# Two more load buffers for the first experts, an identity product for the last group's token sums, and the sample rows normalised in 128 partitions

## The reference, cut to what matters

```python
grp_prob = softmax(tok @ w_gr + b_gr)            # 4 groups of 8 experts, the best group is taken
top_w, top_e = the two best experts in that group
hid = silu(tok @ w_g[e]) * (tok @ w_u[e])        # 32 experts, 2048 -> 256, f32
out = sum over e of combine[:, e] * (hid @ w_d[e])
ple = sigmoid(h @ w_ple_gate) * (p @ w_ple_proj)
x_new = layer_norm(ALPHA * h + out + ple, ln2_g, ln2_b)   # (256, 2048) and (8, 2048)
```

## Time and profile before

| | us |
|---|---|
| median of 3 runs | 1445.55 |
| lowest and highest of them | 1442.3, 1449.25 |
| the profiled execution's own time | 1442.14 |
| its span, first to last instruction | 1440.2 |
| granted TensorE clock, mean of the span | 0.964 |

### The profile page before, as it was taken

The page is one execution under the profiler, slowest core; times in us unless marked ns, Lnnn a source line. Parts: engine busy times, 40 slices in busy tenths (PEclk is TensorE's granted clock), DMA queues, the critical chain, the costliest instruction groups (busy, mean ns, idle before and its releaser), DMA issues.

```text
span 1440.2 us, 21521 instructions
## 1 busy us (share of the span) xinstructions
PE 1320.1 (92%) x8977; PEld 1028.1 (71%) x8977; DVE 762.1 (53%) x1252; ACT 374.4 (26%) x547; POOL 93.9 (7%) x99
## 2 busy tenths in 40 slices
PE   7989999999999999999999998999988799998772
PEld 6989899998788788799999984655543256575320
DVE  4778989898785385465674474012042122211238
ACT  3424333331111211353343462310012020111110
POOL 3840000000010100100100001000000000000000
PEclk9989999999999999999999998999999899999897
DMA  9434444444343633555654649999999999998991
GB/s 249 149 116 154 159 156 147 147 147 144 121 139 127 207 113 108 192 163 187 195 176 147 239 171 357 402 368 403 407 409 408 409 387 398 407 394 321 409 350 71
DMA packets 140534, 351.16 MB, mean 244 GB/s; under 512 B 20808, under 2 KB 21936, under 8 KB 140424
## 3 DMA queue, kind: packets, MB, share of 16 engines
q1 hardware_dynamic: 137168, 339.36, 64.8%
q0 software_dynamic: 3264, 10.37, 2.3%
HBM read 342.52 MB, written 7.18 MB: 243 GB/s over the span
## 4 chain that ended last, share of the span: by engine, by line
PE 69%; DVE 13%; DMA 11%; issue 3%; ACT 2%; SPq 1%; POOL 0%; DVEq 0%; ACTq 0%; POOLq 0%
PE bank L553 67%; DMA mslot<-in_w_exp_up 5%; DMA mslot<-in_w_exp_down 3%; DVE lo L1706 2%; DVE wA L1872 2%; DVE atok L2533 1%; SPq L1247 1%; DVE xpair L1878 1%; ACT hi L1403 1%; DVE wB L1879 1%; DMA raw<-in_w_in 1%; DMA out<-stS 1%; DVE xpair L1881 1%; DVE wA L1891 1%; DMA out<-Sf 1%
## 5 line engine op out<-in xcount | busy, mean ns | idle before, releaser
L1706 DVE TENSOR_TENSOR lo<-raw,hi 128x2048 fp32r<-128x2048 f32 x80 | 188.8, 2361 | 112.0 <-ACT hi L1403 111.5
L1403 ACT ACTIVATE hi<-raw 128x2048 fp32r<-128x2048 f32 x79 | 151.3, 1915 | 258.2 <-PE bank L553 258.2
L553 PE MATMUL bank<-XT,raw 128*128 128x264 f32 x896 | 212.5, 391 | 0.8 <-ACT GA L1500 0.8
L553 PE MATMUL bank<-XH,hi 128*128 128x264 f32 x704 | 206.2, 293 | 5.3 <-DVE lo L1706 5.2
L553 PE MATMUL bank<-XL,hi 128*128 128x264 f32 x704 | 202.0, 287 | 0.0
L553 PE MATMUL bank<-XH,lo 128*128 128x264 f32 x704 | 201.0, 285 | 0.0
L553 PEld LDWEIGHTS bank<-XT,raw 128*128 128x128 f32 x896 | 167.4, 191 | 32.0 <-issue 4.1
L553 PE MATMUL bank<-mslot,Xg 128*32 128x512 f32 (+1 forms) x1024 | 146.9, 663 | 31.5 <-DMA mslot<-in_w_exp_up 31.5
L553 PEld LDWEIGHTS bank<-XH,hi 128*128 128x128 f32 x704 | 134.5, 191 | 11.6 <-DVE lo L1706 7.2
L553 PEld LDWEIGHTS bank<-XL,hi 128*128 128x128 f32 x704 | 134.5, 191 | 0.0
L553 PEld LDWEIGHTS bank<-XH,lo 128*128 128x128 f32 x704 | 134.2, 191 | 0.0
(11 more groups left out here) (421 smaller groups left out, 2101.1 us busy)
## 6 DMA issues: line engine op xcount, KB each, us to landing
raw<-in_w_in SPq DMA_DIRECT2D x72, 1024.0 KB, 5.1
mslot<-in_w_exp_gate SPq DMA_DIRECT2D x128, 512.0 KB, 10.3
mslot<-in_w_exp_up SPq DMA_DIRECT2D x128, 512.0 KB, 12.1
mslot<-in_w_exp_down SPq DMA_DIRECT2D x60, 1024.0 KB, 14.4
raw<-in_w_out SPq DMA_DIRECT2D x16, 1024.0 KB, 5.0
mslot<-in_w_ple_gate SPq DMA_DIRECT2D x16, 1024.0 KB, 13.9
raw<-in_w_branch_b SPq DMA_DIRECT2D x8, 1024.0 KB, 5.0
raw<-in_w_branch_a SPq DMA_DIRECT2D x8, 1024.0 KB, 5.2
```

What stands on the lines that cost most here:

```text
L553: return nc.tensor.matmul(out, w, x, start=start, stop=stop)
L1403: nc.scalar.activation(hi[:, s % RH, :], raw[:, n % RD, :], ACT.Copy).then_inc(hi_done, 1)
L1706: v.tensor_tensor(lo[:, n % RD, :], raw[:, n % RD, :], hi[:, s % RH, :].bitcast(F32), ALU.subtract).then_inc(lo_done, 1)
```

## The change

Four edits:

1. Two buffers are added behind the ten (`EXTRA = 2`), in the space of the second and third tile of `atok`. Chunks 10 and 11 go there, once; from chunk 12 on the ten old buffers are used in turn (`lane`). Chunks 12 to 21 therefore wait for `m_used` to reach two less than before, and later ones for what they waited for before. GpSimd clears `atok` only when 12 chunks have been used, and the filler products `keep_clock` read another buffer.
2. In the last group of the experts TensorE puts the old token sums into the side bank by a product with the identity (`last_scatter`), adds the group's result on top of them, and ScalarE copies the finished sum to `atok` (`copy_sums`); VectorE only takes the statistics (`last_statistics`).
3. The 8 sample rows are spread over 128 partitions (16 to a row) by an SBUF to SBUF transfer `srows<-atok`; their mean and deviation are spread by a small product (`ssel`, `sscal`); two instructions on 128x128 take the place of four on 8x1024.
4. For that, GpSimd's queue issues 17 small loads (`ssel`, 4 KB, and 16 pieces `svecs` of 8 KB each in SBUF) once the last `ple` result has been transposed.

```diff
+EXTRA = 2
...
-        [R_GAB + 8192 * q for q in range(4)] + [R_RAW + 8192 * q for q in range(4)] + [R_HI, R_HI + 8192])]
+        [R_GAB + 8192 * q for q in range(4)] + [R_RAW + 8192 * q for q in range(4)] + [R_HI, R_HI + 8192] +
+        [R_Z + 8192 * (q + 1) for q in range(EXTRA)])]
...
+        def lane(c):
+            return c if c < RM + EXTRA else (c - EXTRA) % RM
-            eng.wait_ge(m_land[c % RM], sum(m_size[x] for x in range(c % RM, c + 1, RM)))
+            eng.wait_ge(m_land[lane(c)], sum(m_size[x] for x in range(c + 1) if lane(x) == lane(c)))
...
-                    mm(bank[0][:, 0:NT], MH[:, i % 4, 0:128], MH[:, i % 4, :], True, True)
+                    mm(bank[0][:, 0:NT], ML[:, i % 4, 0:128], ML[:, i % 4, :], True, True)
...
+            def last_scatter(g, nb):
+                cs = slice(nb * 512, (nb + 1) * 512)
+                if nb == 0:
+                    stored(("st", 0, g))
+                banks = []
+                for tt, (t0, tn) in enumerate(TOK):
+                    banks.append(side(("sc", 0, g, nb, tt)))
+                    stored(("sc", 0, g - 1, nb, tt))
+                    mm(banks[tt][0:tn, :], ident[0:tn, 0:tn], atok[0:tn, tt, cs], True, False)
+                pe.wait_ge(out_low, 4 * g + nb + 1)
+                for tt, (t0, tn) in enumerate(TOK):
+                    mm(banks[tt][0:tn, :], SelT[:, g % 2, t0:t0 + tn], outh[:, nb % 2, :], False, False)
+                    mm(banks[tt][0:tn, :], SelT[:, g % 2, t0:t0 + tn], outl[:, nb % 2, :], False,
+                       True).then_inc(misc_ready, 1)
...
-                down(rnd, groups - 1, lambda nb: scatter(rnd, groups - 1, nb))
+                if rnd:
+                    down(rnd, groups - 1, lambda nb: scatter(rnd, groups - 1, nb))
+                else:
+                    down(rnd, groups - 1, lambda nb: last_scatter(groups - 1, nb))
...
+            def spread_sample_scalars(again):
+                b = side(("samples", again))
+                pe.wait_ge(f_vecs, 16 * 17)
+                pe.wait_ge(f_spread, again + 1)
+                mm(b[:, 0:2], ssel[:, :], sscal[:, :], True, True).then_inc(misc_ready, 1)
+            spread_sample_scalars(0)
+                spread_sample_scalars(1)
...
-                if c >= RM:
+                if c >= 2 * RM + EXTRA:
+                elif c >= RM + EXTRA:
+                    sp.wait_ge(m_used, c - RM - EXTRA + 1)
+                elif c >= RM:
+                    sp.wait_ge(chunk_used, N_END)
...
-                for tt, (t0, tn) in enumerate(TOK):
-                    dst = outs[0][0, t0:t0 + tn, :] if tt < 2 else outs[1].rearrange("b a d -> (b a) d")
-                    for half in range(2 if tt < 2 else 1):
-                        cs = slice(1024 * half, 1024 * (half + 1)) if tt < 2 else slice(0, D)
-                        sp.wait_ge(f_out, 6 * again + (2 * tt + half + 1 if tt < 2 else 6))
+                sp.wait_ge(f_turned, again + 1)
+                sp.dma_start(srows[:, :], atok[0:NB, 2, :]).then_inc(f_small, 16)
+                for tt, (t0, tn) in enumerate(TOK[0:2]):
+                    dst = outs[0][0, t0:t0 + tn, :]
+                    for half in range(2):
+                        cs = slice(1024 * half, 1024 * (half + 1))
+                        sp.wait_ge(f_out, 5 * again + 2 * tt + half + 1)
+                sp.wait_ge(f_out, 5 * again + 5)
+                sp.dma_start(outs[1].rearrange("b a (c j) -> (b a c) j", c=16), syn[:, :]).then_inc(y_out, 16)
...
+            pool.wait_ge(m_used, RM + EXTRA)
+            pool.wait_ge(misc_ready, misc["ple", 3, 2][0] + 1)
+            pool.dma_start(ssel[:, :], t["consts"][0:NB, C_SEL:C_SEL + 128]).then_inc(f_vecs, 16)
+            for i, n in enumerate(("ln2_gain", "ln2_bias")):
+                for b in range(NB):
+                    pool.dma_start(svecs[16 * b:16 * b + 16, i, :], t[n][0].rearrange("(c j) -> c j", c=16)).then_inc(
+                        f_vecs, 16)
...
+            def copy_sums(g, nb):
+                for tt, (t0, tn) in enumerate(TOK):
+                    b, read = side(("sc", 0, g, nb, tt))
+                    nc.scalar.activation(atok[0:tn, tt, nb * 512:(nb + 1) * 512], b[0:tn, :],
+                                         ACT.Copy).then_inc(read, 1)
+            def last_store(g):
+                for nb in range(4):
+                    down_done(act, 0, g, nb)
+                    if nb < 2:
+                        act.wait_ge(misc_ready, misc["sc", 0, g - 1, nb + 2, 2][0] + 1)
+                    nc.scalar.activation(outh[:, nb % 2, :], bank[nb][:, :], ACT.Copy).then_inc(out_high, 1)
+                    if nb:
+                        for done in ((0, 1) if nb == 1 else (nb,)):
+                            copy_sums(g, done)
...
-                store(rnd, groups - 1)
+                if rnd:
+                    store(rnd, groups - 1)
+                else:
+                    last_store(groups - 1)
...
+            def last_statistics(g, nb):
+                for tt, (t0, tn) in enumerate(TOK):
+                    side_read(dve, ("sc", 0, g, nb, tt))
+                    final_link(v.bn_stats(stats[0:tn, tt, nb, :], atok[0:tn, tt, nb * 512:(nb + 1) * 512]))
...
-                scatter(0, g, 0)
-                scatter(0, g, 1)
-                side_read(dve, ("sc", 0, g, 0, 2))
-                side_read(dve, ("sc", 0, g, 0, 1))
-                side_read(dve, ("sc", 0, g, 0, 0))
-                row_statistics(0)
+                last_statistics(g, 0)
+                last_statistics(g, 1)
-                for tt in range(3):
-                    side_read(dve, ("sc", 0, g, 1, tt))
-                row_statistics(1)
-                scatter(0, g, 2)
+                last_statistics(g, 2)
-                for tt in range(3):
-                    side_read(dve, ("sc", 0, g, 2, tt))
-                row_statistics(2)
-                scatter(0, g, 3)
-                row_statistics(3)
+                last_statistics(g, 3)
+                v.memset(told, 0.0).then_inc(f_turned, 1)
...
+                final_link(v.tensor_copy(sscal[:, 0:1], mv[0:NB, 2, 0:1]))
+                v.tensor_copy(sscal[:, 1:2], rstd[0:NB, 2:3]).then_inc(f_spread, 1)
-                for tt, (t0, tn) in enumerate(TOK):
+                for tt, (t0, tn) in enumerate(TOK[0:2]):
...
-                                dve.wait_ge(gained, 6 * again + 2 * tt + half + 1)
+                                dve.wait_ge(gained, 5 * again + 2 * tt + half + 1)
+                b, read = side(("samples", again))
+                v.tensor_copy(sums2[:, :], b[:, 0:2]).then_inc(read, 1)
+                dve.wait_ge(f_small, 16 * again + 16)
+                dve.wait_ge(f_vecs, 16 * 17)
+                side_read(dve, ("samples", again))
+                v.scalar_tensor_tensor(out=syn[:, :], in0=srows[:, :], scalar=sums2[:, 0:1], in1=svecs[:, 0, :],
+                                       op0=ALU.subtract, op1=ALU.mult).then_inc(gained, 1)
+                dve.wait_ge(gained, 5 * again + 5)
+                v.scalar_tensor_tensor(out=syn[:, :], in0=syn[:, :], scalar=sums2[:, 1:2], in1=svecs[:, 1, :],
+                                       op0=ALU.mult, op1=ALU.add).then_inc(f_out, 1)
...
```

More of the change, by code:

```diff
@@ L58 @@
 C_MASK = 400
-C_END = C_MASK + 8 * 128
+C_SEL = C_MASK + 8 * 128
+C_END = C_SEL + 128
 def shape_constants():
@@ L72, in shape_constants @@
     c[:, C_MASK:C_MASK + 128] = np.eye(128)
+    c[0:NB, C_SEL:C_SEL + 128] = r[None, :] // 16 == np.arange(NB)[:, None]
     for n, w in enumerate(LEVELS):
@@ L264, in build @@
     logT = at("logT", R_Z + 40960, [36, NT])
+    srows = at("srows", R_AR + 50272, [P, 128])
+    syn = at("syn", R_AR + 50272 + 512, [P, 128])
+    svecs = at("svecs", R_AR + 50272 + 1024, [P, 2, 128])
+    ssel = at("ssel", R_AR + 49216, [NB, 128])
+    sums2 = at("sums2", R_AR + 49216 + 544, [P, 2])
+    sscal = at("sscal", R_AR + 49216 + 512, [NB, 2])
     wrb = at("wrb", R_AR + 43264, [P, KD, 36])
@@ L331, in build @@
         landed = [sem(f"chunk_landed{s}") for s in range(RD)]
-        m_land = [sem(f"expert_chunk_landed{n}") for n in range(RM)]
+        m_land = [sem(f"expert_chunk_landed{n}") for n in range(RM + EXTRA)]
         hi_done, lo_done, chunk_used = sem("high_done"), sem("low_done"), sem("chunk_used")
@@ L368, in build @@
         gained = sem("gained")
+        f_spread, f_turned, f_small = sem("sample_scalars_ready"), sem("sample_rows_spread"), sem("sample_rows_stored")
+        f_vecs = sem("spread_gain_and_bias_loaded")
         norm_act = sem("normalized")
@@ L933, in ple_gate @@
                     for k in range(4):
-                        last = mm(bank[m][:, 0:NT], mslot[c % RM][:, k * 512 + m * 128:k * 512 + (m + 1) * 128],
+                        last = mm(bank[m][:, 0:NT], mslot[lane(c)][:, k * 512 + m * 128:k * 512 + (m + 1) * 128],
                                   HT[:, 4 * kq + k], kq == 0 and k == 0, kq == 3 and k == 3)
@@ L1225, in ple_load @@
```

(8 more changed lines are left out.)

18 lines of the change are left out of this document (9 added, 9 removed).

## The result

| | us |
|---|---|
| kernel before, median of 8 runs (1440.77 to 1449.25) | 1442.69 |
| changed kernel, median of 8 runs (1433.77 to 1439.02) | 1435.71 |
| ratio, with its 95% interval | 0.9949 [0.9931, 0.9967] |
| profiled execution of the changed kernel, and its span | 1439.02, 1437.2 |

The change makes the kernel 0.5% faster, 7.0 us by these medians. With 8 runs in place of 3 the median of the kernel before is itself 2.9 us lower than the one that the forecast started from.

What follows compares the result with a forecast made beforehand. The prediction took DMA and TensorE in turns as the expert stage's bound, then TensorE, VectorE and the last store. -5.3 + 2.9 + 0.3 - 3.2 + 1.0 = -4.3 us gave 1437.8, plus 3.4: 1441 us, range 1436 to 1447.

Steps and rivals of the forecast that it cites:

- the empty window: Just ahead of the expert stage, 852 to 864 us, DMA share 0.01; two chunks loading there save 5.3 us.
- group 1's first wait: Products at 896.05 us wait for chunks landing 5.3 us earlier; the wait was to stay one for DMA.
- The step at full clock in group 1: Last of the slow steps after waits takes 3.64 us, not 5.34: 1.7 us sooner, so -7.0 us for the buffers.
- The clears: GpSimd's three clears of `atok`, 5.30 us, move some 5 us later, covered by group 0's work: 0.
- the waits were filled as said: In the tail, identity products fill TensorE's three waits ahead of scatters, 1.67 + 1.69 + 1.52 = 4.9 us.
- the upper bound of +3.9 us: Identity sums in the tail: 10.9 us of products, no small waits regained, 0.3 us more of signals.
- The lower bound: Identity sums in the tail: +2.0 us, with 10.2 us of products.
- the first rival: Whole kernel, everything at its good end: -8.2 us, 1437 us; chance 0.20.
- The table load: In the tail, 1.28 us, starting only after the last copy; at most 0.2 us of it shows.
- the rival by which the change is slower: TensorE's clock falls in the tail, from 1400.35 us on; 20.8 us of work doubles, 1462 us; chance 0.04.
- the bound of -3.8 us: Sample rows at the kernel's end: 4.85 us become 1.0 us and the small store does not queue.
- a price by bytes (0.3) and one by packets (2.0): Seventeen small loads near 1325 us: 0.135 MB at 403 GB/s cost 0.3 us, 264 packets cost 2.0 us; +1.0 us taken.

Runs made afterwards that it cites:

- run 9: The changed kernel with one extra buffer (`EXTRA = 1`) in place of two; median 1439.11 us, 1.0 us under the kernel before.
- runs 7 and 11: Changed kernel with the small loads issued after the last group's first down products, 1437.00 us; changed kernel with identity sums for the last 512 columns only, 1430.59 us.
- run 8: The changed kernel with identity sums for the last 512 columns only; median 1431.19 us, 11.5 us under the kernel before.
- run 6: The changed kernel with every identity product issued twice; median 1447.49 us, 4.9 us over the kernel before.
- run 4: The changed kernel with the last group's sums added by VectorE as before, no identity products; median 1434.34 us, 8.4 us under the kernel before.
- run 1: The kernel before with only the two buffers and the clears and fillers that hang on them; median 1438.32 us, 4.4 us under the kernel before.
- Run 5: The changed kernel measured again, unaltered; median 1438.91 us, 3.7 us under the kernel before.

## Why the forecast missed, term by term

The stretches give each term from one trace to the next far better than whole runs, which spread over up to 9 us for one kernel.

| stretch | without the edit | with it | term | forecast |
|---|---|---|---|---|
| group 0's first product to the last group's down piece, two buffers | 534.2, 535.2, 533.6 | 527.4 to 529.3, nine traces, mean 528.3 | -6.0 | -5.3 |
| down piece to aggregate, identity sums | 22.72 | 26.64 | +3.9 | +2.9 |
| aggregate to first step, small copies | 1.27 | 1.40 | +0.1 | +0.3 |
| first step to end of span, sample rows | 19.5, 19.6, 19.5 | 15.1 to 15.4, ten traces, mean 15.3 | -4.2 | -3.2 |
| last step of group 7 to down piece, small loads | 98.0 | 98.1 | +0.1 | +1.0 |
| sum | | | -6.1 | -4.3 |

The last row's stretch lies inside the first one's, so its +0.1 us is counted twice. The first row rests on three traces against nine, which spread over 1.6 and 1.9 us; by it alone -5.3 us can't be ruled out.

**The level.** The forecast added 3.4 us for the median of the three runs over the profiled execution. Eight runs put that at 1442.69 - 1442.14 = 0.6 us. This is the largest single error, -2.9 us, and the step that failed: the forecast set a difference of 3.4 us, taken from a median of three, on top of its sum, and it measured 0.6. With the right level the forecast's own sum would have given 1437.8 + 0.6 = 1438.4 us. The terms were off by another 1.8 us, which gives 1436.6 us. Their sum of -6.1 us lies between the two comparisons of the same pair, -7.0 and -3.7 us; what is left, 0.9 us, is less than their distance. Of the terms, sample rows (1.0 us), small loads (0.9), buffers (0.7) and copies (0.2) came out better than forecast, the identity sums 1.0 us worse; that last error hid part of the miss.

**The two buffers: mechanism right, size perhaps a little short.** They load in the empty window, group 1's first wait stays a wait for DMA, and it ends 5.1 us sooner in the mean of the nine traces (28.5 against 33.6 us behind group 0's start), as worked out; run 9 halves it. About 0.7 us more come by the last down piece; single executions vary by up to 1 us around the mean, so I don't put it down to one cause. The step at full clock in group 1 that I listed for -7.0 us happened in the profiled execution (904.63, 3.64 us) and in runs 7 and 11, in the six other traces with both buffers it took its 5.2 to 5.3 us. It is a matter of the execution. At the last down piece the three are 0.9 us ahead of the six, not 1.7. In the profiled one the gain was taken back: from 1277 to 1287 us the clock fell, and 1.7 us went. Run 11 kept it, reached the fourth step of group 7 3.3 us sooner than run 8 (427.4 against 430.7 us behind group 0's start) and the last down piece only 1.1 us sooner (527.4 against 528.5): from there on the full queue sets the pace (share 1.02 from 1320 to 1392 us). The clears started 4.8 us later behind group 0's start and nobody waited, as said. (The prediction's "steps of 32 products" are 32 instructions, 16 products.)

**The identity sums: the waits were filled as said, the term mis-sized.** It came out at the upper bound of +3.9 us. The price of a product was 0.957 us in place of 0.874, 12 x 0.083 = 1.0 us, all of it on the path, since TensorE had no gap left. I scaled a row of products of one form by its columns, and for such products the price holds: 0.86 us each in run 6. What I put at nothing is the tenth of a microsecond at each change of form, up to three of them in each of the four sets. The lower bound was wrong as well: 10.2 us of products give 10.2 - 4.9 - 0.3 - 2.4 = +2.6 us, not +2.0, which makes the first rival -7.6 us; and no row gives the 10.2. Behind the last scatter it was 1420.50 - 1418.86 = 1.6 us, forecast 1.5. The table load didn't show: it ended at 1420.80 us, and ScalarE then waited for VectorE. The clock stayed at 1.00, so the rival by which the change is slower didn't come in.

**The sample rows: what was foreseen came as forecast, and 0.8 us more.** Even the bound of -3.8 us was too small. VectorE's part came as worked out, 1.02 us in place of 4.85. I had then added 0.6 us, 1.3 at most, for a small store that queues behind the last large one. It did queue, for 1.28 - 0.77 = 0.5 us, the same in all ten traces that have it, which makes -3.3 us, the forecast's -3.2. What I put at nothing is the time from the small store's last packet to the end of the span: 3.9 to 4.0 us in the three traces of the old form (8 packets of 8192 bytes), 2.8 to 3.2 us in the ten of the new one (128 packets of 512 bytes). Why it is shorter is open; a run that changes only the small store's form or its place in the queue was not made.

**The small loads: a term too large.** +1.0 us was between a price by bytes (0.3) and one by packets (2.0). The stretch with and without them shows 0.1, within its spread of 1 us, and their packets took 0.63 us of the 16 engines; both are under the forecast. The price by packets was taken from unlike loads: the 384 packets of the earlier trace rows hold a load of 256 KB, and the view counts 544 packets for the seventeen loads, not 264. The Trainium skill (DMA: Bandwidth & Descriptors, Bandwidth, Measured) has transfers under 64 KB dominated by their descriptors; by its 0.68 us each the estimate was 11.6 us, and no run here shows that: the measured 0.1 us, and 0.63 us of engine time for all seventeen, speak against adding it up beside a full weight queue.

**What the change would be without its bad part.** Runs 4 and 10 are one kernel (no identity sums), 8.4 and 9.0 us faster than before; runs 8 and 11 are another (identity sums in the last quarter alone), 11.5 and 9.5 us faster. The second has the lowest medians here, 1431.19 and 1430.59 us, and by its stretch of the tail it is 1.0 us ahead of the first.

## What to carry to other kernels

Fill an engine's waits with other work only up to the length of the waits: twelve products, 11.4 us in all, put into 4.9 us of waits lost 3.9 us even with 2.3 us regained behind them, while three of them at the one place where they also shorten the chain behind gained 1.0 us. Here a buffer more was worth the bytes that it let into an idle stretch of the queue, whichever wait it ended. A price scaled from products of one form leaves out what a change of form adds, here up to 0.1 us each time. Where runs of a kernel spread over 0.5%, take the level from many runs and the terms from stretches between two fixed instructions, never from a difference of two spans.

## What I had not expected of the hardware

The clock granted to TensorE fell while it was busy throughout. Windows after:

```profile
1267.00:1277.00 10.00, 10.00 (x69) 6.40 (x68) 0.00 (x0) 0.31 (x1) 0.00 (x0) 1.00 1.03 407
1277.00:1287.00 10.00, 10.00 (x45) 8.31 (x45) 0.00 (x0) 3.51 (x10) 0.00 (x0) 0.83 1.03 397
```

and of run 4, at nearly the same place in the work (its third step of group 7 starts 1.8 us later):

```profile
1276.00:1286.00 10.00, 10.00 (x65) 8.03 (x58) 0.00 (x0) 3.82 (x10) 0.00 (x0) 1.00 1.04 400
```

PE is busy for 10.00 of 10 us in each. The lower clock cost 1.7 us between the third and fourth step of group 7 (23.3 against 21.6 us); run 1 shows it too, the others not. In groups 0 and 1 a step of 32 instructions takes 3.64 us at full clock and 5.2 to 6.6 us where the low clock covers part of it, and which steps get which differs between executions of the same kernel. Nor is it always the step behind a wait, as the prediction had it. Run 5 is the changed kernel again, and the fourth step of its group 0, with no wait ahead, is the slow one:

```profile
881.65 5.34 PE L569 MATMUL bank<-mslot,Xg 128*32 128x512 f32 x32
888.88 3.64 PE L569 MATMUL bank<-mslot,Xg 128*32 128x512 f32 x32 [0.28 <-DMA mslot<-in_w_exp_up]
```

How much of the spread of the runs this explains is not shown.
